# Attention steps of a fused diffusion block: the output products of step k-1 ahead of both transpose rounds of step k

## The chip, the cores and the metric

The kernel runs on one core of a Trainium2 chip, which is one core of eight. The metric is the device time of the whole kernel in microseconds, the median of repeated runs; lower is better. Engines are named as the profile has them: PE is TensorE (PEld its weight loads), DVE is VectorE, ACT is ScalarE, POOL is GpSimd, SP is SyncE, which here only issues DMAs.

## The reference

Two layers over 512 latent tokens with a context of 256 tokens ahead of them, model width 1024, everything in fp32. Each layer projects its normed input, runs two kinds of attention beside each other, joins their outputs in one projection, and then runs a gated feed-forward part with a short convolution. Four kinds of attention occur: in layer 0 MLA (8 heads, latent keys with a rotary part, 768 rows of queries, context included) and SWA (8 heads, window of 128 keys, a sink logit); in layer 1 NA (8 heads, neighbourhood attention on a grid with a relative bias) and GQA (4 heads of 128), both with 512 rows of queries. Cut to what all four share:

```python
s = jnp.einsum('bgrqd,bgkd->bgrqk', q, k_all).astype(jnp.float32) * scale
p = jax.nn.softmax(s, axis=-1)          # SWA: a sink logit more; NA: bias and mask
o = jnp.einsum('bgrqk,bgkd->bgrqd', p, v_all)
```

## The kernel before

The whole program is one launch with an instruction list per engine, written out by hand; semaphores with counted values tie the lists together. Each engine runs its list in order. The change lies in the attention phases, which all come out of the same function, `attention(name, a)`, once on each engine.

**Steps.** A phase works on pairs of heads, and for each pair on units of 128 query rows. A step k is one unit of one pair: MLA and SWA have 4 pairs with 6 units (24 steps), NA 4 pairs with 4 units (16), GQA 2 pairs with 4 units (8). In MLA's units 0, 2, 4 and 5 of a pair all 768 keys are seen (six tiles of 128), in units 1 and 3, which are context rows, only 256 keys. SWA's units see 512, 256, 640, 256, 640 and 512 keys. NA's and GQA's all see 768. The index x is the head within the pair.

**What a step takes, and who does it.**

- Scores, TensorE (`scores`, L1030 in GQA, L1038 elsewhere, L1045 for MLA's rotary part), into PSUM banks 0 to 3, two banks for each head. These banks exist once, so the scores of step k+2 overwrite those of k+1.
- Row minima of the negated scores, VectorE (`minima`, L1866, in NA two passes, L1855 and L1866). They write a copy of the scores to SBUF as well; `mx_done` counts them, and the scores of the next step wait for both of them.
- Exponent with row sum, ScalarE (`exp`, L1442), the reciprocal of the sum, VectorE (L1871), and the scaling of the row, GpSimd (L2180, `p_scaled`).
- Transposes of the scaled probabilities, TensorE (`probs_t`, through `turns`, L993). A round handles one head: its left half of key tiles goes to bank 6, its right half to bank 7. Bank 6 is copied to SBUF by ScalarE (L1425), bank 7 by VectorE (L1830), and the next round's halves wait for `left_free` and `right_free`, each for the copy of its own bank.
- The output product, TensorE (`pv`, L1075), from the transposed probabilities and the values. It waits for both copies of the second round of its step.
- Preparation of the next pair (`prep`): rounds of transposes of q, k and, in MLA and GQA, a third operand, through the same two banks. They follow the transposes of units 1, 2, 3 (MLA), 1, 2 (SWA), 0, 1 (NA) and 0, 1, 2 (GQA).

**The order of the work.** TensorE's list has for step k: scores of k+1, first round of k (x = 0), output product of k-1, second round of k (x = 1), then preparation. At k = 0 there is no output product; after the loop the output product of the last step follows. VectorE's list for the same k is: minima of k+1 for head 0, copy of round (k, 0), minima of k+1 for head 1, reciprocal of k+1 for head 0, (at the first unit of a pair the low part of the finished pair's output), copy of round (k, 1), reciprocal for head 1. ScalarE's: copy of round (k, 0), exponent of k+1 for head 0, (at the first unit of a pair the finished pair's output), copy of round (k, 1), exponent for head 1.

Of the kernel before, what the change touches and what calls it, by code (L numbers as in the profile page):

```python
# [118 lines left out]
def keys_of(unit):  # L119
    _, (a, n), (b, m) = unit  # L120
    return [*range(a, a + n), *range(b, b + m)]


def build(nc, I, C, out):
# [16 lines left out]
    with ctx:  # L141
# [284 lines left out]
        def at_least(eng, sem, value):  # L426

            if not (isinstance(value, int) and value <= 0):
                eng.wait_ge(sem, value)
# [371 lines left out]
        def _(pe):  # L801
# [182 lines left out]
            def attention(name, a):  # L984
# [3 lines left out]
                def turns(r, left, right):  # L988

                    for srcs, b, done, free in ((left, 6, left_done, left_free), (right, 7, right_done, right_free)):  # L990
                        at_least(pe, free, R0 + r)
                        for n, src in enumerate(srcs):
                            last = nc.tensor.transpose(bank(b)[:, n * P:(n + 1) * P], src, ident[:, :])  # L993
                        last.then_inc(done, 1)
# [8 lines left out]
                def prep(p, i):  # L1003
                    what, (left, right) = a.preps[i]
                    if a.name == "mla" and what == "x" and p == 0:
                        turns(a.prep_round[p, i], [x_first[:, t, :] for t in left], [x_first[:, t, :] for t in right])
                        return
                    turns(a.prep_round[p, i], [raw_tile(what, p % 2, t) for t in left],
                          [raw_tile(what, p % 2, t) for t in right])

                def prep_in(p):
                    pe.wait_ge(head_in[p % 2], head_fills[name] + (p // 2 + 1) * a.load_inc)
# [35 lines left out]
                def probs_t(k, x):  # L1048
                    p, u = a.steps[k]
                    n = len(keys_of(a.units[u]))  # L1050
                    pe.wait_ge(p_scaled, S0 + 2 * k + x + 1)
                    v = (sunk if a.name == "swa" else biased)[k % 2][x][:, ROWS - n * P:ROWS]
                    srcs = [v[:, c * P:(c + 1) * P] for c in range(n)]
                    turns(a.unit_round[k, x], srcs[:(n + 1) // 2], srcs[(n + 1) // 2:])

                def pv(k):
                    p, u = a.steps[k]
                    s, t = p % 2, a.units[u][0]
                    keys = keys_of(a.units[u])
                    r = R0 + a.unit_round[k, 1] + 1  # L1060
                    pe.wait_ge(left_free, r)
                    pe.wait_ge(right_free, r)
                    if u == 0:
                        pe.wait_ge(v_in[s], v_fills[name] + (p // 2 + 1) * a.v_inc)
                        at_least(pe, o_lo, OL0 + H0 + (p - 1 if a.name == "na" else p))
                    v = v_raw[s].rearrange("p (t c) -> p t c", t=NT)
                    for c, key in enumerate(keys):
                        for x in range(2):
                            if a.name == "gqa":
                                o, w = bank(4 + x), v[:, key, :]  # L1070
                            else:
                                b = 4 + s if a.name == "na" else 4
                                o = ps[64 * x:64 * x + 64, b * 512:b * 512 + a.acols]
                                w = v[:, key, 0:64] if a.name == "swa" else v[:, key, 64 * x:64 * x + 64]
                            last = mm(o[:, t * P:(t + 1) * P], w, pt[k % 2][x][:, c, :],  # L1075
                                      start=c == 0, stop=c == len(keys) - 1)
                    last.then_inc(pv_done, 1)
# [11 lines left out]
                for k in range(-1, last_step + 1):  # L1089
                    if k < last_step:  # L1090
                        p, u = a.steps[k + 1]
                        if u == 0:
                            pe.wait_ge(left_free, R0 + a.prep_end(p))
                            pe.wait_ge(right_free, R0 + a.prep_end(p))
                        at_least(pe, mx_done, S0 + 2 * (k + 1))
                        scores(k + 1)
                    if k < 0:
                        continue
                    probs_t(k, 0)
                    if k:  # L1100
                        pv(k - 1)
                    probs_t(k, 1)
                    p, u = a.steps[k]
                    for i in range(len(a.preps)):
                        if a.prep_at[i] == u and p + 1 < a.pairs:
                            if i == 0:
                                prep_in(p + 1)
                            prep(p + 1, i)
# [174 lines left out]
            first_norm_turns()  # L1283
            in_projection(0)
            attention("mla", MLA)
            attention("swa", SWA)
            out_projection(0)
            feed_up(0)
            feed_down(0)
            into_projection()  # L1290
            in_projection(1)
            attention("na", NA)
            attention("gqa", GQA)
            out_projection(1)
# [973 lines left out]
```

## Time and profile before

| | us |
|---|---|
| median of 3 runs (lowest, highest) | 1861.03 (1859.75, 1861.37) |
| the profiled execution, its span | 1856.1, 1854.4 |
| TensorE busy, share of the span | 1706.3, 92% |
| VectorE, ScalarE, GpSimd busy | 1019.9, 645.6, 267.3 |
| L993, all transposes through `turns` in attention, matmuls | 141.1 |
| L1171, feed-forward products of layer 0 and 1 | 830.0 in three groups |

The span is the time from the first to the last instruction in the profile; the execution's own time lies 1.7 us above it. The time runs from the input projections of layer 0 (until about 188 us) through MLA (to 316) and SWA (to 411), the feed-forward part of layer 0, the projections of layer 1, NA (1264 to 1354), GQA (to 1421) and the feed-forward part of layer 1. A start in a timeline row is when an instruction began to run on its engine, and rows of one kind that follow each other are merged (x6). For a matmul the duration includes filling and draining of the array, so a merged row ends a little after the next may start; from start to start is the better measure.

### The profile page before, as it was taken

What the parts mean: (1) busy time and instruction counts of PE and PEld (TensorE: products, weight loads), DVE (VectorE), ACT (ScalarE), POOL (GpSimd) and SP (SyncE); (2) the same over time, 40 slices, a digit from 0 to 9 for tenths busy, and PEclk for the clock granted to TensorE, in tenths of its full rate; (3) what the DMA queues carried; (4) which work ended last, traced back from release to release, by engine and by line L of the source; (5) the groups of instructions that cost most, each with busy time, mean ns of one, the idle gap of its engine ahead of it and who ended that gap; (6) DMA issues with size and microseconds to landing.
All of it is one profiled execution on the core that took longest, in us unless ns stands there. A gap on an engine that the chain in (4) does not pass through costs nothing.

```text
span 1854.4 us, 27146 instructions
## 1 busy us (share of the span) xinstructions
PE 1706.3 (92%) x10042; PEld 1366.3 (74%) x10042; DVE 1019.9 (55%) x1927; ACT 645.6 (35%) x1089; POOL 267.3 (14%) x396
## 2 busy tenths in 40 slices
PE   5898898989989999999996969998989799999998
PEld 1876565668878888888785857885667598888886
DVE  3656455754657777776653482156743634443445
ACT  2424455653321212212223332235643433233343
POOL 0414222320200000000010030125521200000001
PEclk9999999999989999999998989998999899999999
DMA  8479441114514343344254542354502523332233
GB/s 300 162 256 322 77 106 44 24 38 158 172 46 121 106 136 116 111 136 126 70 126 116 173 153 96 130 154 104 139 10 80 158 70 90 91 109 72 80 125 136
DMA packets 258270, 224.21 MB, mean 121 GB/s; under 512 B 67484, under 2 KB 218411, under 8 KB 258178
## 3 DMA queue, kind: packets, MB, share of 16 engines
q1 hardware_dynamic: 249156, 202.50, 36.3%
q0 software_dynamic: 7008, 18.79, 3.5%
q10 hardware_dynamic: 2016, 1.71, 0.3%
q8 instruction: 58, 0.95, 0.2%
q14 instruction: 32, 0.26, 0.0%
HBM read 193.71 MB, written 29.25 MB: 120 GB/s over the span
## 4 chain that ended last, share of the span: by engine, by line
PE 80%; DVE 6%; DMA 4%; ACT 3%; issue 3%; SPq 2%; POOL 2%; ACTq 0%; DVEq 0%
PE ps L1171 29%; PE ps L806 10%; PE ps L808 10%; PE ps L807 10%; PE ps L993 5%; PE ps L1075 4%; PE ps L1038 4%; PE ps L1181 1%; DMA w_raw<-in_ffn_down 1%; PE ps L1030 1%; PE ps L863 1%; PE ps L1045 1%; ACT arena L1425 1%; PE ps L1155 1%; DMA wide_raw<-in_ada_w 1%
## 5 line engine op out<-in xcount | busy, mean ns | idle before, releaser
L806 PE MATMUL ps<-w_hi,act_hi 128*128 128x512 f32 (+2 forms) x952 | 370.1, 389 | 21.8 <-DVE act_lo L1614 18.6
L1614 DVE TENSOR_TENSOR w_lo<-w_raw,w_hi 128x2048 fp32r<-128x2048 f32 (+3 forms) x114 | 209.5, 1838 | 310.7 <-ACT w_hi L1316 310.7
L808 PE MATMUL ps<-w_hi,act_lo 128*128 128x512 f32 (+2 forms) x952 | 366.2, 385 | 0.0
L807 PE MATMUL ps<-w_lo,act_hi 128*128 128x512 f32 (+2 forms) x952 | 366.2, 385 | 0.0
L1316 ACT ACTIVATE w_hi<-w_raw 128x2048 fp32r<-128x2048 f32 (+3 forms) x110 | 172.4, 1568 | 308.3 <-PE ps L808 249.2
L1171 PE MATMUL ps<-act_lo,w_hi 128*128 128x512 f32 (+1 forms) x912 | 278.3, 359 | 0.0
L1171 PE MATMUL ps<-act_hi,w_hi 128*128 128x512 f32 (+1 forms) x912 | 277.1, 358 | 0.0
L1171 PE MATMUL ps<-act_hi,w_lo 128*128 128x512 f32 (+1 forms) x912 | 274.6, 355 | 0.0
L806 PEld LDWEIGHTS ps<-w_hi,act_hi 128*128 128x128 f32 x952 | 180.9, 190 | 62.1 <-issue 23.3
L808 PEld LDWEIGHTS ps<-w_hi,act_lo 128*128 128x128 f32 x952 | 180.3, 189 | 34.4
L807 PEld LDWEIGHTS ps<-w_lo,act_hi 128*128 128x128 f32 x952 | 180.6, 190 | 33.5
L1171 PEld LDWEIGHTS ps<-act_hi,w_lo 128*128 128x128 f32 x912 | 151.5, 189 | 27.8
L1171 PEld LDWEIGHTS ps<-act_hi,w_hi 128*128 128x128 f32 x912 | 149.4, 188 | 29.7 <-issue 4.5
L1171 PEld LDWEIGHTS ps<-act_lo,w_hi 128*128 128x128 f32 x912 | 150.7, 189 | 24.6
L993 PE MATMUL ps<-ident,arena 128*128 128x128 f32 x882 | 141.1, 290 | 27.4 <-ACT arena L1425 14.3
L993 PEld LDWEIGHTS ps<-ident,arena 128*128 128x128 f32 x882 | 96.8, 144 | 76.1 <-issue 30.2
L1515 ACT ACTIVATE arena<-ps,conv 128x768 f32<-128x768 f32 (+1 forms) x44 | 39.0, 886 | 313.5 <-PE ps L1171 290.0
L2180 POOL TENSOR_SCALAR arena<-arena,rinv 128x768 f32<-128x768 f32 (+3 forms) x144 | 111.6, 776 | 241.0 <-DVE rinv L1871 241.0
L1669 DVE SCALAR_TENSOR_TENSOR arena<-arena,silu 128x256 f32<-128x256 f32 x336 | 137.1, 478 | 0.9
L1425 ACT ACTIVATE arena<-ps 128x384 f32<-128x384 f32 (+2 forms) x179 | 78.2, 437 | 138.4 <-PE ps L993 135.6
L1442 ACT ACTIVATE arena<-arena,nb 128x768 f32<-128x768 f32 (+4 forms) x144 | 115.4, 801 | 23.8 <-DVE nb L1866 23.3
L1932 DVE SCALAR_TENSOR_TENSOR arena<-ps,conv,arena 128x511 f32<-128x511 f32 x66 | 41.6, 658 | 121.9 <-ACT arena L1515 121.9
(129 smaller groups left out, 2008.2 us busy)
## 6 DMA issues: line engine op xcount, KB each, us to landing
arena<-in_ada_w SPq DMA_DIRECT2D x44, 1024.0 KB, 9.3
w_raw<-in_ffn_up SPq DMA_DIRECT2D x88, 512.0 KB, 5.1
w_raw<-in_ffn_down SPq DMA_DIRECT2D x88, 256.0 KB, 3.0
w_raw<-in_odd_w_in SPq DMA_DIRECT2D x20, 512.0 KB, 4.9
arena<-mods SPq DMA_DIRECT2D x16, 512.0 KB, 7.3
proj_odd<-arena POOLq DMA_DIRECT2D x26, 256.0 KB, 2.7
x_after_mix<-arena SPq DMA_DIRECT2D x10, 512.0 KB, 2.9
arena<-x_after_mix SPq DMA_DIRECT2D x10, 512.0 KB, 5.0
```

The costliest lines, as they stand in the source:

```text
L806: mm(out_, s_hi, m_hi, start=start, stop=False)
L807: mm(out_, s_hi, m_lo, start=False, stop=False)
L808: return mm(out_, s_lo, m_hi, start=False, stop=stop)
L993: last = nc.tensor.transpose(bank(b)[:, n * P:(n + 1) * P], src, ident[:, :])
L1038: last = mm(out_of(x, off, n), qt[s][h, rows], kt[s][h, keys], start=True, stop=not rope)
L1171: last = mm(o, wt[:, k, :], m[:, k, rows], start=st, stop=sp_)
L1316: A(w_hi[:, s, 0:n], w_raw[:, s, 0:n], ACT.Copy).then_inc(w_hi_done, 1)
L1425: A(dst, bank(6, n * P), ACT.Copy).then_inc(left_free, 1)
L1442: A(dst, src, ACT.Exp, bias=nb[:, s, x:x + 1], scale=-1.0, accum_out=rsum[:, s, x:x + 1])\
L1614: V.tensor_sub(out_, full, hi.bitcast(fp32)).then_inc(sem_, 1)
L1669: ins = V.scalar_tensor_tensor(out=ada_sum[:, v, :], in0=w, scalar=x, in1=ada_sum[:, v, :], op0=ALU.mult, op1=ALU.add)
L2180: Q.tensor_scalar(v, v, rinv[:, k % 2, x:x + 1], 1.0, ALU.mult, ALU.mult).then_inc(p_scaled, 1)
```

## The change

In TensorE's list of each attention step the output product of step k-1 moves ahead of the first round of transposes of step k, so that both rounds of step k follow each other. All waits move with the instructions they belong to. The lists of the other four engines are the same, instruction by instruction.

```diff
                         scores(k + 1)
                     if k < 0:
                         continue
-                    probs_t(k, 0)
                     if k:
                         pv(k - 1)
-                    probs_t(k, 1)
+                    for x in range(2):
+                        probs_t(k, x)
                     p, u = a.steps[k]
```

TensorE's list in MLA, the stretch from the short scores of unit 1 to the short scores of unit 3, before. L1038 and L1045 are scores, L993 transposes, L1075 output products (two heads for each key tile).

```order
L1038 MATMUL ps<-arena 128x128 x4
L1045 MATMUL ps<-arena 128x128 x4
L993 MATMUL ps<-ident,arena 128x128 x6
L1075 MATMUL ps<-arena 64x128 x12
L993 MATMUL ps<-ident,arena 128x128 x6
L1038 MATMUL ps<-arena 128x384 x4
L1045 MATMUL ps<-arena 128x384 x4
L993 MATMUL ps<-ident,arena 128x128 x2
L1075 MATMUL ps<-arena 64x128 x12
L993 MATMUL ps<-ident,arena 128x128 x8
L1038 MATMUL ps<-arena 128x128 x4
L1045 MATMUL ps<-arena 128x128 x4
```

The same stretch now:

```order
L1038 MATMUL ps<-arena 128x128 x4
L1045 MATMUL ps<-arena 128x128 x4
L1075 MATMUL ps<-arena 64x128 x12
L993 MATMUL ps<-ident,arena 128x128 x12
L1038 MATMUL ps<-arena 128x384 x4
L1045 MATMUL ps<-arena 128x384 x4
L1075 MATMUL ps<-arena 64x128 x12
L993 MATMUL ps<-ident,arena 128x128 x10
L1038 MATMUL ps<-arena 128x128 x4
L1045 MATMUL ps<-arena 128x128 x4
```

Before, the twelve products stood between two rounds of six transposes; now the two rounds are one run of twelve. In the second step the two short rounds (2 and 2) and a preparation round (6) join to a run of ten.

The end of NA, where the last step has no next scores, before:

```order
L1038 MATMUL ps<-arena 128x512 x2
L1038 MATMUL ps<-arena 128x256 x2
L993 MATMUL ps<-ident,arena 128x128 x6
L1075 MATMUL ps<-arena 64x128 x12
L993 MATMUL ps<-ident,arena 128x128 x12
L1075 MATMUL ps<-arena 64x128 x12
L993 MATMUL ps<-ident,arena 128x128 x6
L1075 MATMUL ps<-arena 64x128 x12
```

The end of NA now:

```order
L1038 MATMUL ps<-arena 128x512 x2
L1038 MATMUL ps<-arena 128x256 x2
L1075 MATMUL ps<-arena 64x128 x12
L993 MATMUL ps<-ident,arena 128x128 x12
L1075 MATMUL ps<-arena 64x128 x12
L993 MATMUL ps<-ident,arena 128x128 x12
L1075 MATMUL ps<-arena 64x128 x12
```

The run of twelve before was the second round of step 14 and the first of step 15. Now the product of step 14 stands between them, and the two rounds of step 15 stand together.

## Rows read from the trace of the kernel before

**Rows 1.** The page's chain that ended last, shares of the span by engine.

```profile
PE 80%; DVE 6%; DMA 4%; ACT 3%; issue 3%; SPq 2%; POOL 2%; ACTq 0%; DVEq 0%
```

**Rows 2.** Busy us (instructions) per engine, the four attention stretches together.

```profile
sum 380.90, PE 344.21 PEld 240.25 DVE 224.22 ACT 207.81 POOL 128.65; mean PE 86.05 PEld 60.06 DVE 56.05 ACT 51.95 POOL 32.16
```

**Rows 3.** Timeline of an MLA step: start us, us, engine, line, operation [idle before].

```profile
225.04 0.88 PE L993 MATMUL ps<-ident,arena 128*128 128x128 f32 x6
...
225.84 1.53 PE L1075 MATMUL ps<-arena 128*64 128x128 f32 x24
...
226.03 0.55 DVE L1830 COPY arena<-ps 128x384 f32<-128x384 f32 x1
226.14 0.94 ACT L1442 ACTIVATE arena<-arena,nb 128x768 f32<-128x768 f32 x1
226.50 0.95 DVE L1866 CUSTOM_DVE_ANT_0 arena<-ps,band 128x768 f32<-128x768 f32 x1
...
227.31 0.88 PE L993 MATMUL ps<-ident,arena 128*128 128x128 f32 x6
...
228.11 0.72 PE L1038 MATMUL ps<-arena 64*128 64x128 f32 x8
228.29 0.56 DVE L1830 COPY arena<-ps 128x384 f32<-128x384 f32 x1 [0.77 <-PE ps L993]
```

**Rows 4.** Timeline, MLA: a preparation round of transposes directly behind T1.

```profile
240.54 0.88 PE L993 MATMUL ps<-ident,arena 128*128 128x128 f32 x6
...
241.73 0.95 PE L993 MATMUL ps<-ident,arena 128*128 128x128 f32 x6 [0.31 <-ACT arena L1425]
```

**Rows 5.** Timeline, start of GQA: the second scores wait for the minima.

```profile
1360.94 0.96 DVE L1866 CUSTOM_DVE_ANT_0 arena<-ps,band 128x768 f32<-128x768 f32 x1 [0.32 <-PE ps L1030]
...
1361.96 2.85 PE L1030 MATMUL ps<-arena 128*128 128x384 f32 x8 [1.06 <-DVE nb L1866]
```

**Rows 6.** Timeline, end of an MLA pair, where the output product is short.

```profile
250.70 0.88 PE L993 MATMUL ps<-ident,arena 128*128 128x128 f32 x6
...
252.09 0.87 PE L993 MATMUL ps<-ident,arena 128*128 128x128 f32 x6
252.16 0.95 DVE L1866 CUSTOM_DVE_ANT_0 arena<-ps,band 128x768 f32<-128x768 f32 x1
...
253.26 1.20 PE L1038 MATMUL ps<-arena 64*128 64x384 f32 x5 [0.29 <-ACT arena L1425]
```

**Rows 7.** Timeline, an SWA step with 512 keys.

```profile
344.17 0.42 DVE L1830 COPY arena<-ps 128x256 f32<-128x256 f32 x1
...
344.68 0.75 DVE L1866 CUSTOM_DVE_ANT_0 arena<-ps,band,arena 128x512 f32<-128x512 f32 x1
...
345.14 0.66 PE L993 MATMUL ps<-ident,arena 128*128 128x128 f32 x4
...
345.72 0.70 PE L1038 MATMUL ps<-arena 64*128 64x256 f32 x4
345.90 0.42 DVE L1830 COPY arena<-ps 128x256 f32<-128x256 f32 x1 [0.39 <-PE ps L993]
```

**Rows 8.** Timeline, an NA step.

```profile
1288.96 0.87 PE L993 MATMUL ps<-ident,arena 128*128 128x128 f32 x6
...
1290.20 0.55 DVE L1830 COPY arena<-ps 128x384 f32<-128x384 f32 x1
...
1290.67 0.68 DVE L1855 CUSTOM_DVE_ANT_0 arena<-ps,arena 128x512 f32<-128x512 f32 x1
...
1292.03 1.56 PE L1038 MATMUL ps<-arena 64*128 64x512 f32 x8
```

**Rows 9.** Transposes (L993): TensorE idle before them until this releaser: us, times.

```profile
  POOL arena L2180: 20.4, 42
```

**Rows 10.** Stretches of 4 us, with granted clock (PEclk) behind the engines.

```profile
1264.00:1268.00 4.00, 2.93 (x8) 1.28 (x8) 0.80 (x2) 1.76 (x2) 4.00 (x2) 0.50 0.02 8
...
1352.00:1356.00 4.00, 2.81 (x34) 2.14 (x32) 1.25 (x2) 1.63 (x5) 0.00 (x0) 1.00 0.04 8
```

## The prediction, as it was put on record

> **What bounds the kernel now.** I read the page's chain by engine first [rows 1]: TensorE carries 80% of the chain that ended last, and the other engines appear in it in small pieces. The change touches one Python loop that four attention phases run, so the second view is the busy table of these four stretches [rows 2]: together 380.9 us, of which TensorE is busy 344.2, or 90%. Attention is TensorE's own time with small gaps; VectorE is busy 224.2 us there (59%), ScalarE 207.8, GpSimd 128.7. No engine beside TensorE is near its limit, so whatever else decides is latency: how long the chain from one TensorE instruction through VectorE or ScalarE back to TensorE takes, and whether TensorE has other work meanwhile.
>
> The third view is the timeline of one step [rows 3]. Name the parts of a step k: S is the scores of step k+1, T0 and T1 the two rounds of transposes of step k, O the output product of step k-1. Before, TensorE runs T0 at 225.04, O at 225.84, T1 at 227.31 and the next S at 228.11. T0 to S is 3.07 us: 0.80 + 1.47 + 0.80, with no gap. What lies beside it: T0's right half is copied by VectorE at 226.03, and behind that copy, in VectorE's program order, stand the row minima of the second head of step k+1, at 226.50. The next S overwrites the banks that these minima read, so it must wait for them. Behind O (1.47 us) both copies and minima are hidden.
>
> **What the change does to a step.** TensorE's instruction count and kinds stay the same; the orders of the other four engines and of all DMAs are unchanged. No wait is added in the code, but two are met in another situation.
>
> First, T1 writes the banks that T0 just filled, so it must wait for ScalarE's copy of T0's left half. Before, O stood between them. How long two rounds need back to back is shown where a preparation round follows T1 [rows 4]: start to start 1.19 us (240.54 to 241.73), against 0.80 for a round without the wait. That is +0.39 per step, the lower price.
>
> Second, and dearer: T0 now starts 1.47 us later, and VectorE, which runs in order, holds the minima of the second head behind T0's copy. From T0 to the next S the chain is: T0's start to VectorE's copy 0.98 us (227.31 to 228.29, where VectorE was free [rows 3]); copy to minima 0.47 us (226.03 to 226.50 [rows 3]); minima to the scores that waited for them 1.02 us (1360.94 to 1361.96 [rows 5]). Sum 2.47 us. Two rounds and their gap need only 1.19 + 0.80 = 1.99 us, so the minima end last and S starts 2.47 us after T0. The step is O 1.47 + 2.47 = 3.94 against 3.07: **+0.87 us**. ScalarE's part of it fits inside: its exponent starts 1.10 after T0 (226.14 less 225.04 [rows 3]) and is 0.94 long, so its second copy starts near 2.1 and nothing on TensorE waits for it unless a preparation round follows.
>
> MLA has 24 steps, 23 of them with an O in the loop (k = 1 to 23). By what step k and step k+1 are (long: 768 keys; short: 256):
> - Long to long with a long O: 3 steps, 3 x 0.87 = 2.6.
> - Long to long with a short O (0.59 us): 4 steps. Here the kernel before already waits: T0 at 250.70, T1 at 252.09 (so O is 1.39 - 0.80 = 0.59), minima at 252.16, S at 253.26, 0.37 after TensorE came free [rows 6]. The row's label names ScalarE's copy, but the code lets this S wait for no such copy, only for the minima, whose end fits too. T0 to S is 2.56; after, 0.59 + 2.47 = 3.06, so +0.50; 4 x 0.5 = 2.0 (the last includes the drain: there the product of the step before now fills the wait for the last scaled probabilities, and two copies become exposed behind it; I count these as equal).
> - Long to short: minima of 256 columns are short, so the lower price rules: 7 x 0.39 = 2.7.
> - Short to long, mostly followed by a preparation round: the preparation needs both ScalarE copies, and between them stands an exponent of 0.94 us [rows 3]. Between 0.39 and 0.87 by the rows above plus this; I take 0.75, nearer the upper end, since minima and exponent are both long ones: 8 x 0.75 = 6.0.
> Sum for MLA 13.3.
>
> SWA: 23 steps. A step with 512 keys on both sides [rows 7]: a round takes 0.58 (345.14 to 345.72), so T0 to S was 1.16 beside O. After: a round's start to its copy is 0.76 (345.14 to 345.90), copy to minima 0.51 (344.17 to 344.68, a sink copy lies between), the minima 0.75 and 0.06 from their end to S as in rows 5: 2.08. Hence +0.92 for the 3 such steps, 2.8. For the rest I carry MLA's prices: 4 steps with a short O at 0.5, halved since these minima are shorter, 1.0; 7 long to short at 0.5 (0.39 and a little for the sink copies), 3.5; 8 short to long at 0.75, 6.0. At the start of each later pair the finished pair's output is evicted by ScalarE and then by VectorE in front of T1's copies. The scores are short here, so O, now first, meets that eviction where T0 took up part of it; 3 x 0.5 = 1.5, an estimate between nothing and 1 us. The drain 0.5. Sum 15.3.
>
> NA: 16 steps, all long, and the minima are two passes [rows 8]: before, T0 at 1288.96, S at 1292.03, 3.07 again. The second head's first pass starts 0.47 after the copy (1290.20 to 1290.67) and S follows 1.36 later (1292.03). After: 0.98 + 0.47 + 1.36 = 2.81, and with O 4.28: +1.21. Of the 15 steps with an O, 9 have no preparation behind them and a next step: 10.9; the last one is the drain, counted as nothing by the same exchange as in MLA. 5 have one: there the kernel before already pays 0.39, and the preparation's right half waits for a copy queued behind the same minima; between 0.82 (1.21 - 0.39) and 1.21 I take 0.95: 4.8. Sum 15.7; 1292.03 is also when TensorE came free, so 1.36 may be a little too long.
>
> GQA: 7 steps with O, one-pass minima like MLA, all long; O is longer but hides more than was needed. At 0.87 to 1.21 I take 1.0: 7.0.
>
> **The sum.** 13.3 + 15.3 + 15.7 + 7.0 = 51.3, with the rows' rounding 52 us. Saved against it: TensorE's waits for GpSimd's scaled probabilities, at most 20.4 us over the whole kernel [rows 9]; most of that is at starts and drains, which the terms above hold. In a step's middle T0 follows S with no gap before ([rows 3]: 225.04), so putting O ahead frees nothing there. Everything behind attention waits for its last output and moves by the same amount. The profiled execution took 1856.1 us (span 1854.4 and 1.7 around it); with 52 it is 1908. The median of the three timed runs is 1861.0, 4.9 above the profiled one, so the forecast is **1913 us**, +2.8%.
>
> **The clock.** A weight on the other side of the sum is TensorE's clock. Rows of this case show it at half its level (0.50, that is 1.2 of 2.4 GHz) at 1264 to 1268, after TensorE was mostly idle, while 1352 to 1356, busy 2.81 of 4 us, ran at full clock [rows 10]. After the change a long step is busy about 5.4 of 6.3 us, 86%, above what kept full clock. The Trainium skill ("TensorE: Matmul & The Clock Gate", A second HAM failure mode: psum-queue depth-cycling) says that short idle spells between groups of matmuls that cycle through PSUM banks can make the clock swing between its two levels. This case's trace does not show it at such gaps.
>
> **The rivals.**
> - The lower price only: VectorE's minima stay hidden and T0 to T1 costs 0.39 in all 68 steps (23 + 23 + 15 + 7): 26.5 us, 1888. For it: the rounds' wait is the only bank conflict that the code shows at first sight. Against it: VectorE's order is fixed and rows 6 show TensorE already waiting for the minima when O is short. Chance 0.10.
> - Faster: the output product fills TensorE's waits for scaled probabilities, and the copies keep pace since VectorE and ScalarE are under 60% busy. Place: S to T0 in every step, and the drains. Price: the 20.4 us of [rows 9] go, and it decides if T1 finds its bank free within the 0.80 us of T0. 1861 - 20 = 1841. Against it: rows 4 show 1.19. Chance 0.02; for it to cancel exactly (no change) 0.02.
> - The clock swings: TensorE's work in attention, 344 us, runs at half clock for a fifth of the time. At half clock a round of fixed length doubles, so 69 us are added to the 52: 1982. Against it the row of 1352. Chance 0.06, and dearer or cheaper in proportion.
> - My forecast, the minima behind the later copy: 0.80. Its own range is 1901 to 1924, from the bounds of the estimated terms: at 0.39 for all 8 short-to-long steps of MLA or of SWA and nothing for SWA's evictions the sum is 47; at 1.0 for the steps of one of the two, 1.21 for all of NA's steps and for GQA's it is 56; and some 7 us more at each end for rows carried from one phase to another and for the median of the runs.
>
> **How the numbers follow.** The range reaches a little towards the first and the third rival: 1895 to 1928. A measurement of this kernel tells about 0.2% (4 us) from no change. Slower: 0.80 + 0.10 + 0.06 = 0.96; within 0.2%: 0.02; faster: 0.02.
>
> **What would show it.** In the changed profile a long MLA step should read O, T0, a gap of 0.4, T1, a gap of about 0.5 ended by the minima (L1866), then S, with S 2.47 us after T0 and a period of 6.3 instead of 5.4 us. VectorE's busy time stays while TensorE's idle time in attention doubles or more, and the four stretches grow by about 13, 15, 16 and 7 us. The first step of each phase keeps its length. Wrong would be: S within 2.1 us of T0 (then VectorE took its copy earlier than I think, and the first rival holds), or a granted clock below 1 in the middle of a phase (the third), or T0 to T1 of 0.80 (the second).

## The result, and the profile after

The changed kernel takes 1917.35 us (median of 4 runs, 1909.91 to 1922.99), the kernel before, on the same chip, 1860.39 (4 runs, 1858.86 to 1861.37). The ratio is 1.030, with a 95% interval of 1.0278 to 1.0321: 57 us slower. The forecast was 1913 us in a range of 1895 to 1928. The profiled execution took 1915.25 us, 59.2 more than that of before. All ratios in this document leave out one run of the kernel before, on the chip of e1, e2, e3 and e5, which took 3389.49 us.

The chain of the changed kernel that ended last, by engine, answers to [rows 1]:

```profile
PE 78%; DVE 7%; DMA 4%; ACT 4%; issue 3%; POOL 2%; SPq 1%; DVEq 0%; ACTq 0%
```

TensorE gives two points to VectorE and ScalarE. How much that is shows in the four attention stretches (MLA, SWA, NA, GQA), with busy us (instructions) of each engine, then the granted clock, the DMA share and GB/s. The last row answers to [rows 2], whose stretches were cut 5.6 us wider than the phases:

```profile
195.06:339.15 144.09, 121.53 (x1123) 79.21 (x1123) 70.25 (x206) 65.00 (x161) 36.77 (x48) 0.97 0.24 56
339.15:447.04 107.89, 83.86 (x724) 56.50 (x724) 62.77 (x217) 56.06 (x154) 31.67 (x48) 0.97 0.09 20
1298.00:1408.46 110.46, 87.53 (x749) 58.92 (x749) 62.22 (x203) 52.15 (x113) 45.69 (x40) 0.94 0.31 80
1408.46:1478.77 70.31, 59.03 (x366) 45.34 (x367) 28.29 (x69) 25.47 (x53) 14.54 (x16) 1.00 0.00 1
sum 432.75, PE 351.94 PEld 239.97 DVE 223.53 ACT 198.68 POOL 128.67; mean PE 87.99 PEld 59.99 DVE 55.88 ACT 49.67 POOL 32.17
```

Cut in the same way, at the first scores of each phase, the kernel before reads 127.50, 91.01, 93.35 and 63.44 us, 375.3 together, with TensorE busy for 340.1 and VectorE for 223.5. The phases grow by 16.6, 16.9, 17.1 and 6.9 us, 57.5 together; all the rest of the span by 1.7. VectorE does the same work. TensorE's idle time in attention goes from 35.2 us (375.3 less 340.1) to 80.8 (432.8 less 351.9), so 45.6 of the 57.5 us are waits. The other 11.9 us are busy time of the same instructions: in part the stretches at half clock that are told below, where scores that take 1.56 us at full clock took 2.93, and the rest is not traced further.

A long MLA step of the changed kernel, from its timeline, answers to [rows 3]: O, T0, T1, S, with the copies and the minima of the second head.

```profile
232.05 1.53 PE L1075 MATMUL ps<-arena 128*64 128x128 f32 x24
...
233.51 0.88 PE L993 MATMUL ps<-ident,arena 128*128 128x128 f32 x6
234.16 0.49 ACT L1425 ACTIVATE arena<-ps 128x384 f32<-128x384 f32 x1 [3.54 <-PE ps L993]
234.49 0.56 DVE L1830 COPY arena<-ps 128x384 f32<-128x384 f32 x1 [1.37 <-PE ps L993]
...
234.79 0.86 PE L993 MATMUL ps<-ident,arena 128*128 128x128 f32 x6 [0.40 <-ACT arena L1425]
234.97 0.95 DVE L1866 CUSTOM_DVE_ANT_0 arena<-ps,band 128x768 f32<-128x768 f32 x1
...
235.98 0.49 PE L1038 MATMUL ps<-arena 64*128 64x128 f32 x4 [0.32 <-DVE nb L1866]
```

The three links of the forecast chain stand there: 0.98 us from T0 to VectorE's copy, 0.48 to the minima, 1.01 to S; together 2.47. T0 to T1 is 1.28 us. VectorE sat idle for 1.37 us before its copy: it waited for T0, which stood behind the whole of O, and had nothing else to do in its order.

An NA step of the changed kernel, from its timeline, answers to [rows 8]:

```profile
1326.25 0.88 PE L993 MATMUL ps<-ident,arena 128*128 128x128 f32 x6
...
1327.23 0.56 DVE L1830 COPY arena<-ps 128x384 f32<-128x384 f32 x1 [1.14 <-PE ps L993]
...
1327.70 0.68 DVE L1855 CUSTOM_DVE_ANT_0 arena<-ps,arena 128x512 f32<-128x512 f32 x1
...
1328.98 1.56 PE L1038 MATMUL ps<-arena 64*128 64x512 f32 x8 [0.58 <-DVE nb L1866]
```

S starts 2.73 us after T0 here, and 2.83 in the step before it (1320.47 to 1323.30). The idle time before the transposes by releaser, over the whole changed kernel, answers to [rows 9]:

```profile
  ACT arena L1425: 59.3, 118
...
  POOL arena L2180: 4.1, 10
```

This view counts TensorE's weight loads together with its matmuls, and a weight load may wait while a matmul still runs; so it is no measure of TensorE's lost time. The matmuls alone stand on the pages, the kernel before first:

```profile
L993 PE MATMUL ps<-ident,arena 128*128 128x128 f32 x882 | 141.1, 290 | 27.4 <-ACT arena L1425 14.3
L993 PE MATMUL ps<-ident,arena 128*128 128x128 f32 x882 | 141.1, 290 | 55.7 <-ACT arena L1425 44.9
```

The transposes themselves waited for ScalarE's copy 32 times before (14.3 us) and 98 times after (44.9 us): T1 met the bank wait 66 times more, for 30.6 us. For GpSimd they waited 5 times before, 3.7 us in all, and 2 times after, 0.5 us; the 20.4 us of [rows 9] are for the greater part weight loads (16.8 in 37 waits). The scores waited for the minima (L1866) 4 times before, 7.6 us, and 28 times after, 19.6 us, and the products for VectorE's copies 3.1 and 7.9 us. So of the new waits the bank is the larger part (30.6 us), the minima behind the late copy the smaller (12.0): where both stand in one step, the minima add only what the bank wait has not already covered.

Last, the clock. Windows of 4 us of the changed kernel at the first step of MLA, in NA's second pair, and at the start of SWA, with columns as in [rows 10]:

```profile
192.00:196.00 4.00, 3.33 (x15) 2.21 (x15) 0.00 (x0) 1.96 (x4) 0.00 (x0) 0.50 1.05 206
...
332.00:336.00 4.00, 2.79 (x35) 2.25 (x33) 1.11 (x2) 0.98 (x2) 0.00 (x0) 1.00 0.01 4
336.00:340.00 4.00, 2.74 (x24) 2.02 (x20) 1.02 (x2) 2.45 (x5) 0.00 (x0) 1.00 0.24 50
340.00:344.00 4.00, 1.94 (x12) 1.02 (x8) 2.45 (x10) 1.80 (x5) 1.39 (x2) 0.87 0.88 196
344.00:348.00 4.00, 3.80 (x15) 1.97 (x16) 1.73 (x8) 1.58 (x6) 0.96 (x2) 0.50 0.00 0
...
1332.00:1336.00 4.00, 2.29 (x16) 1.58 (x16) 2.95 (x9) 3.43 (x8) 3.00 (x2) 1.00 0.33 99
1336.00:1340.00 4.00, 4.00 (x24) 2.19 (x24) 1.33 (x4) 0.04 (x1) 2.94 (x2) 0.57 0.00 0
```

At the start of SWA the granted clock is 0.87 in the stretch from 340 to 344, in which TensorE was busy 1.94 us, and 0.50 (1.2 of 2.4 GHz) in the next. In NA it is 0.57 from 1336 to 1340, behind a stretch with 2.29 us busy. The stretches from 332 to 340, the drain of MLA, busy 2.7 to 2.8 us, ran at full clock.

**Step by step.** From the start of one step's scores to the start of the next one's, in us, read from the timelines. The interval holds these scores and all that follows them to the next; "long O" and "short O" say how long the output product in it is, and the forecast's growth stands beside it. The columns e1 to e7 belong to the experiments below.

| interval | forecast | before | after | e1 | e2 | e4 | e7 |
|---|---|---|---|---|---|---|---|
| MLA, long to long, long O | +0.87 | 5.42 | 6.28 | 5.89 | 5.89 | 5.42 | 5.62 |
| MLA, long to long, short O | +0.50 | 4.91 | 5.49 | 5.30 | 5.01 | 5.30 | 5.28 |
| MLA, long to short | +0.39 | 4.15 | 4.61 | 4.61 | 4.61 | 4.15 | 4.31 |
| MLA, short to long, preparation | +0.75 | 5.81 | 6.51 | 6.52 | 6.20 | 5.82 | 5.95 |
| SWA, 512 keys on both sides | +0.92 | 3.48 | 4.40 | 3.93 | 4.04 | 3.65 | 3.75 |
| NA, no preparation | +1.21 | 4.57 | 5.68 | 5.03 | 5.28 | 4.96 | 5.03 |
| NA, preparation of unit 0 | +0.95 | 6.09 | 7.17 | 7.10 | 7.61 | 6.12 | 6.52 |
| GQA, no preparation | +1.0 | 6.57 | 7.77 | 7.18 | 7.19 | 6.58 | 6.57 |

### The profile page after: what moved, and what is told of

It is laid out like the page before. It is cut to its first block, busy times and chain, and to the rows that moved or that the text cites. A ratio compares the mean times of both kernels' runs of the same rounds, so it can differ in the third digit from the quotient of the medians.

```text
span 1913.6 us, 27146 instructions
## 1 busy us (share of the span) xinstructions
PE 1717.3 (90%) x10042; PEld 1368.8 (72%) x10042; DVE 1019.6 (53%) x1927; ACT 640.2 (33%) x1089; POOL 267.5 (14%) x396
## 4 chain that ended last, share of the span: by engine, by line
PE 78%; DVE 7%; DMA 4%; ACT 4%; issue 3%; POOL 2%; SPq 1%; DVEq 0%; ACTq 0%
PE ps L1171 28%; PE ps L806 10%; PE ps L807 10%; PE ps L808 10%; PE ps L1075 5%; PE ps L993 4%; PE ps L1038 4%; PE ps L1181 1%; DMA w_raw<-in_ffn_down 1%; ACT arena L1425 1%; DVE arena L1830 1%; PE ps L1030 1%; DVE arena L1866 1%; PE ps L1045 1%; PE ps L863 1%
## 5 line engine op out<-in xcount | busy, mean ns | idle before, releaser
L993 PE MATMUL ps<-ident,arena 128*128 128x128 f32 x882 | 141.1, 290 | 55.7 <-ACT arena L1425 44.9
L993 PEld LDWEIGHTS ps<-ident,arena 128*128 128x128 f32 x882 | 96.4, 145 | 95.9 <-issue 62.4
L1830 DVE COPY arena<-ps 128x384 f32<-128x384 f32 (+2 forms) x168 | 79.3, 472 | 100.3 <-PE ps L993 100.0
```

The source lines that it names most:

```text
L1830: V.tensor_copy(dst, bank(7, n * P)).then_inc(right_free, 1)
```

## The experiments

Eight runs on three chips; each ratio is against runs of the kernel before on the same chip (medians there 1863.28 for e1, e2, e3 and e5, 1865.53 for e4, e7 and e8, 1859.61 for e9).

### e1: the changed kernel, VectorE's second minima ahead of its copy of T0

```diff
                     if k < last_step:
                         minima(k + 1, 0)
+                        minima(k + 1, 1)
                     for x in range(2):
                         if k >= 0:
                             probs(k, x)
-                        if x == 0 and k < last_step:
-                            minima(k + 1, 1)
```

> The changed kernel, with one edit on VectorE: the row minima of the second head of step k+1 stand ahead of the copy of the first transpose round of step k, instead of behind it. My theory is that the 57 us lost have two parts: the second round waits for its bank (T0 to T1 1.28 us instead of 0.80), and the next scores wait for minima queued behind a copy that now comes late (T0 to S 2.47 us in MLA, 2.8 in NA). This edit takes away the second part where no preparation round follows: T0 to S should fall to 1.28 + 0.80 = 2.08 us, worth 0.39 in 7 MLA steps, about 0.3 in 12 SWA steps, 0.7 in 9 NA steps and 0.4 in 5 GQA steps, together some 15 us: 1902 (1895 to 1908). Rival 1, only the bank wait counts and the minima are hidden: 1917, no change. Rival 2, the loss is TensorE's clock: the time follows the granted clock and not this edit, 1917 as well. Rival 3, the minima are the whole loss: near 1865.

Measured: 1898.14 us (1896.32 to 1900.57), ratio 1.0187 (1.0170 to 1.0204), inside the 1895 to 1908 expected. By the ratios 22 of the 57 us came back by VectorE's order alone; by the traces the phases shrank by 18.0 us, of which 1.4 are one NA step that ran at half clock in the changed kernel. Its timeline of the long MLA step:

```profile
267.18 0.95 DVE L1866 CUSTOM_DVE_ANT_0 arena<-ps,band 128x768 f32<-128x768 f32 x1
267.65 0.87 PE L993 MATMUL ps<-ident,arena 128*128 128x128 f32 x6
...
268.93 0.86 PE L993 MATMUL ps<-ident,arena 128*128 128x128 f32 x6 [0.40 <-ACT arena L1425]
...
269.72 0.72 PE L1038 MATMUL ps<-arena 64*128 64x128 f32 x8
```

The minima now run beside O, where VectorE was idle, and S follows T1 with no wait: T0 to S is 2.07 us, 1.28 + 0.79. The bank wait of 0.40 is what remains. The table's first row splits so: 6.28 - 5.89 = 0.39 for the minima, 5.89 - 5.42 = 0.47 for the bank. In NA it is 0.65 and 0.46. The short-to-long steps did not move (6.51, 6.52): there the preparation waits for copies, not for the minima. The page of this run has 44.3 us of bank waits before the transposes, where the changed kernel's has 44.9: e1 removes one part and leaves the other.

### e2: the kernel before, the product behind both rounds

```diff
-                    probs_t(k, 0)
+                    for x in range(2):
+                        probs_t(k, x)
                     if k:
                         pv(k - 1)
-                    probs_t(k, 1)
```

> The kernel before, with the output product of step k-1 behind both transpose rounds of step k instead of between them. Both rounds follow each other as in the changed kernel, but T0 starts right after the scores, so VectorE's copy and minima come as early as in the kernel before and lie beside the product. It prices the bank wait alone. My theory: 0.48 us for each step without a preparation round (14 in MLA, of which 4 with a short product at 0.1; 17 in SWA; 10 in NA; 5 in GQA), next to nothing in the 23 with one, since the product then stands where that round waited: 1860 + 20 = 1880 (1874 to 1886). Rival 1, the bank wait is the whole loss: 1917. Rival 3, it costs nothing and the minima are everything: 1861.

Measured: 1891.40 us (1889.71 to 1893.36), ratio 1.0147 (1.0130 to 1.0164). The long MLA step:

```profile
232.47 0.87 PE L993 MATMUL ps<-ident,arena 128*128 128x128 f32 x6
...
233.75 0.86 PE L993 MATMUL ps<-ident,arena 128*128 128x128 f32 x6 [0.41 <-ACT arena L1425]
...
234.55 1.53 PE L1075 MATMUL ps<-arena 128*64 128x128 f32 x24
...
236.01 0.72 PE L1038 MATMUL ps<-arena 64*128 64x128 f32 x8
```

T0 again comes straight behind the scores and the minima are hidden beside O, so this is the bank wait alone: T0 to S is 3.54 us against 3.07, +0.47, as expected. The growth was expected at 20 us and came out at 28 (1891.40 against 1863.28). I had taken the steps with a preparation as free of it, and some are not: MLA's short-to-long ones went from 5.81 to 6.20, while its long-to-short ones with a preparation stayed at 4.55, and GQA's two read 7.62 for 7.73 and 8.70 for 8.70. In NA the steps without a preparation grew by 0.71 and not by 0.47. There the minima are two passes, so VectorE's copy of T0 comes later, and the right half of T1 waits for it too; T1's row is 1.12 us long for 0.86:

```profile
1320.23 0.88 PE L993 MATMUL ps<-ident,arena 128*128 128x128 f32 x6
...
1321.51 1.12 PE L993 MATMUL ps<-ident,arena 128*128 128x128 f32 x6 [0.40 <-ACT arena L1425]
...
1325.26 0.41 PE L993 MATMUL ps<-ident,arena 128*128 128x128 f32 x2 [1.17 <-ACT arena L1425]
```

The last row, the preparation of unit 0 of a pair in NA (6.09 to 7.61), waits for something else again, the order of ScalarE's list, which e8 below shows. So 27 us, by the ratio, is the price of this order in this kernel: the bank wait for the greater part, with these two beside it. It is no price that holds wherever the product stands; e1, with the product ahead and the minima hidden, lies 35 us above the kernel before.

### e3: the change in layer 0 only

```diff
+                    first = a.full
+                    if k and first:
+                        pv(k - 1)
                     probs_t(k, 0)
-                    if k:
+                    if k and not first:
                         pv(k - 1)
                     probs_t(k, 1)
```

> The change in the two attention phases of layer 0 alone (MLA and SWA); NA and GQA keep the order of the kernel before. From the two traces MLA grew by 16.6 us and SWA by 16.9. If the loss is local to each step, as my theory has it, this kernel shows just these: 1860.4 + 33.5 = 1894 (1889 to 1899). A rival in which the slower attention of one layer delays something that the other layer waits for (a transfer, the clock) would leave the sum short or long of that by more than 5 us.

Measured: 1892.94 us (1890.16 to 1895.10), ratio 1.0153 (1.0137 to 1.0170). MLA and SWA took 143.45 and 107.78 us, as in the changed kernel, NA and GQA 93.59 and 63.43, as before. The four phases together are 33.0 us longer than before, and 33.5 were expected. The medians say 29.7 us (1892.94 less 1863.28), some 4 less, just inside the 5 us that the expectation allowed. The loss is local to each phase; nothing in NA, GQA or behind them is seen to give it back or to add to it.

### e4: the kernel before, with e1's order on VectorE

The edit on VectorE is that of e1; TensorE's order is that of the kernel before.

> The kernel before, with VectorE's second minima put ahead of its first copy out of PSUM: the same edit that gave e1 back 19 us, in a kernel whose TensorE order is not changed. Theory (the order of VectorE suits the order of TensorE; with the old TensorE order the minima have 3.07 us of cover and the copy of T0's round is what the next round of the bank waits for): T1's right half waits for a copy that now stands behind both minima, and so does the product; MLA long steps +0.1, MLA short ones +0.6, NA steps +0.6, so 10 to 20 us slower than before, 1871 to 1883. Rival (the minima-first order is better in itself, and e1 tells nothing of the change): 1863 or less, down to about 1845.

Measured: 1875.47 us (1872.64 to 1877.31), ratio 1.0049 (1.0031 to 1.0067), 9 us slower. The rival falls: the minima-first order is no better in itself, it costs 9 us with one order of TensorE and saves 22 with the other. The size lay at the lower edge of the 10 to 20 us that I had expected, since the MLA steps with a long O lost nothing (5.42), and those with a short O and NA's lost 0.39 and not 0.6. Where it bites, an MLA step with a short O:

```profile
227.93 0.55 PE L993 MATMUL ps<-ident,arena 128*128 128x128 f32 x3
...
228.40 0.55 DVE L1830 COPY arena<-ps 128x384 f32<-128x384 f32 x1
...
229.01 0.55 PE L993 MATMUL ps<-ident,arena 128*128 128x128 f32 x3 [0.53 <-DVE arena L1830]
```

The left half of T1 goes, and the right half waits 0.53 us for the copy that now stands behind the minima.

### e5: the kernel before, the product in two halves around T1

If two rounds with nothing between cost 0.4 us, the round of a preparation that follows T1 costs that in the kernel before too [rows 4]. Here half of the product stands between them. Only steps with a preparation are cut, and not the first of a pair; `pv` takes the first or the second half of the key tiles.

```diff
+                    p, u = a.steps[k]
+                    parted = p + 1 < a.pairs and u in a.prep_at[:len(a.preps)] and u > 0
                     probs_t(k, 0)
                     if k:
-                        pv(k - 1)
+                        pv(k - 1, 0 if parted else None)
                     probs_t(k, 1)
+                    if k and parted:
+                        pv(k - 1, 1)
```

> The kernel before, with one edit: in the steps that a preparation round follows (20 with an output product and not the first of a pair) the product of step k-1 is cut in two halves by key tiles, one between T0 and T1, one between T1 and the preparation. By the theory, what stands between two rounds hides the 0.39 us wait for the copy; the kernel before leaves that wait open in front of each preparation. Half a long product is 0.73 us, more than 0.39, half a short one 0.3. Expected gain 0.2 to 0.39 us for each of the 20, less where ScalarE's exponent holds up its second copy: 3 to 8 us, 1855 (1852 to 1858). Rival (the wait in front of a preparation is hidden by something else, or VectorE's queue sets it): 1860, no change.

Measured: 1856.41 us (10 runs, 1852.75 to 1860.93), ratio 0.9972 (0.9962 to 0.9982). A parted MLA step (L1078 is the product's line in this kernel):

```profile
235.63 0.44 PE L993 MATMUL ps<-ident,arena 128*128 128x128 f32 x2
236.00 0.88 PE L1078 MATMUL ps<-arena 128*64 128x128 f32 x12
236.80 0.48 PE L993 MATMUL ps<-ident,arena 128*128 128x128 f32 x2
237.22 0.88 PE L1078 MATMUL ps<-arena 128*64 128x128 f32 x12
238.07 0.85 PE L993 MATMUL ps<-ident,arena 128*128 128x128 f32 x6
238.84 0.71 PE L1038 MATMUL ps<-arena 64*128 64x128 f32 x8
```

No wait is left, and T0 to S is 3.21 us against 3.46. The same in the table's terms: short to long with a preparation 5.81 to 5.55, and long to short with a preparation 4.54 to 4.42.

### e7: half of the product ahead of T0, half between T0 and T1

```diff
+                    if k:
+                        pv(k - 1, 0)
                     probs_t(k, 0)
                     if k:
-                        pv(k - 1)
+                        pv(k - 1, 1)
                     probs_t(k, 1)
```

> After, but every output product is cut in two by keys: half of it is issued ahead of T0 and half between T0 and T1, and nothing between T1 and the scores. Theory (the loss has two parts: nothing between the two rounds, so T1 waits 0.39 us and more for the copies of T0's banks, and nothing between T1 and S, so S waits for T0 to minima, 2.47 us in MLA and 2.83 in NA): half a product of 0.74 us covers the bank wait whole, and T0 to S of 2.34 us of TensorE's own work nearly meets the 2.47 us chain; MLA about +4, SWA +5, NA +6, GQA +2 against before, total about 1880 (1872 to 1890). Rival A (what counts is that T0, and with it the copies and minima, starts late behind any part of a product): about half of the whole loss stays, 1889 or more. Rival B (only the bank wait matters): 1866 or less.

Measured: 1884.37 us (1882.41 to 1886.33), ratio 1.0103 (1.0085 to 1.0120). The phases grew by 4.8, 6.9, 5.9 and 0.4 us. Both rivals fall. With half a product between them T0 and T1 start 1.61 us apart with no bank wait. In the step of the table's first row T0 starts at 229.39 and S at 231.85, 2.46 us, near the forecast's 2.47. TensorE's own work between them is 2.41 us, so only 0.05 of this is the chain through the minima. The +0.20 of the interval is half a product (0.81) ahead of T0, and 2.46, against 3.07 before; 0.15 of it is the cut itself, since two halves of 0.81 us stand where a whole product took 1.47. In MLA this run therefore says little about the chain. In NA it says more:

```profile
1331.70 0.87 PE L993 MATMUL ps<-ident,arena 128*128 128x128 f32 x6
...
1334.43 1.56 PE L1038 MATMUL ps<-arena 64*128 64x512 f32 x8 [0.24 <-DVE nb L1872]
```

T0 to S is 2.73 us, the same as in the changed kernel, with no bank wait and with 2.41 us of TensorE's own work; the scores wait for the minima (L1872 in this kernel).

### e8: e5 also at the first step of a pair

The condition `u > 0` of e5 is dropped.

> e5 (before, with the product cut in two around T1 where a preparation follows) extended to the first step of a pair, which e5 left whole; only NA and GQA prepare there, 7 and 3 times. Theory (T1 to the preparation is 1.28 us there and would be 0.80 if half a product stood between): 0.4 us a time, 4 us less than e5, so about 0.9955 of before (1853 where before is 1861). Rival (the preparation's own copies on ScalarE set the length of these steps): the same as e5, 0.997 of before.

Measured: 1865.08 us (12 runs, 1861.20 to 1870.66), ratio 1.0000 (0.9989 to 1.0011). Neither the theory's 0.9955 nor the rival's 0.997: these steps became longer, 7.04 us against 6.09 in NA. There are two of them with a product, where I had written seven: NA has four pairs, so three preparations, and the first falls into a step with no product. What the changed wait hangs on shows in ScalarE's rows of such a step, of e5 first:

```profile
1294.25 0.60 ACT L1466 ACTIVATE act_hi<-ps 128x512 fp32r<-128x512 f32 x1
1294.78 0.49 ACT L1433 ACTIVATE arena<-ps 128x384 f32<-128x384 f32 x1
```

and of e8, with the second half of the product and the preparation on TensorE:

```profile
1303.10 0.88 PE L1078 MATMUL ps<-arena 128*64 128x128 f32 x12
...
1305.14 0.41 PE L993 MATMUL ps<-ident,arena 128*128 128x128 f32 x2 [1.17 <-ACT arena L1433]
```

```profile
1304.02 0.60 ACT L1466 ACTIVATE act_hi<-ps 128x512 fp32r<-128x512 f32 x1 [0.95 <-PE ps L1078]
1304.51 0.48 ACT L1433 ACTIVATE arena<-ps 128x384 f32<-128x384 f32 x1
```

At the first step of a pair ScalarE's list has the output of the finished pair (L1466) ahead of the copy of T1 (L1433). The output needs the product's last half, which now comes behind T1, so ScalarE waits 0.95 us for it and T1's copy waits with it; then the preparation waits 1.17 us for that copy. This is the same fault as in the change: an instruction put behind another on TensorE delays, through the order of a second engine, something that did not depend on it. The 2.9 us that e8's trace has more than e5's in MLA do not come from the edit: there both run the same instructions, and e8's first long step ran at half clock (the scores at 205.66 took 2.93 us instead of 1.56). The two longer steps explain 1.9 us, 0.1%; the ratio lies 0.28% above that of e5, and what makes up the rest is not shown.

### e9: e5 once more

> The kernel of e5 once more, with runs of the kernel before on the same chip, since e8, which runs the same instructions in MLA and SWA, took 2.9 us more in MLA (its first step ran at half clock) and its ratio was 1.000. Theory (the parted product saves 0.4 us a pair in MLA and about as much in NA and GQA, some 3 us in all, and e8 lost it in NA, where ScalarE's copy of T1 came 1.2 us late behind the output of the pair): 0.9985 of before (0.997 to 0.9995). Rival A (0.9972 of e5 was the edit's own doing): 0.9972 again. Rival B (e5's gain was the clock's luck): 1.000.

Measured: 1857.44 us (12 runs, 1850.23 to 1860.51), ratio 0.9984 (0.9972 to 0.9996). The theory's value, but its working was too low: step by step e5 and e9 agree within 0.02 us behind the first steps of the phases, and against before they save 0.56 us in each of three MLA pairs (0.25 + 0.12 + 0.19, and not 0.4), 0.3 in SWA, 1.0 in NA (three parted steps) and 1.3 in GQA (7.73 to 7.01 and 8.71 to 8.09). That is 4.3 us, or 0.9977, which lies in the intervals of both e5 and e9. Rival B falls; rival A is not excluded, since 0.9972 is the edge of this run's interval. The parted product is the one version here that beats both kernels, by some 0.2%, at the edge of what can be told.

## Why the prediction was right

**The chain through the minima held, link by link.** The first rows of the table are the forecast's terms: +0.86 for +0.87, +0.58 for +0.50, +0.46 for +0.39, +0.70 for +0.75, SWA's +0.92 exactly. NA came out at +1.11 to +1.20 for +1.21 (from the first pass of the minima to S it took 1.28 us in the step shown, for 1.36), and its steps with a preparation at +0.86 and +1.08 for +0.95. GQA was +1.10 to +1.20 in the steps without a preparation and +0.74 in those with one, for +1.0 throughout. e1 and e7 show the cause and not only the size: take the minima from behind the copy and MLA's 0.39 goes; take the bank wait away and NA's 2.73 stays.

**Bank wait.** It was carried at 1.19 us from start to start and is 1.28 in every long step, so 0.47 where 0.39 stood. [Rows 4] measured a preparation behind T1; why that is 0.09 shorter was not tried. In the long-to-long steps this did not matter, since the minima end later; in the seven long-to-short steps of MLA it is the term that was too small, by 0.07 each. The two short-to-long steps of MLA's last pair, which no preparation follows, were carried at 0.75 with the others and grew by 1.02.

**The sum.** Forecast 51.3 us, measured 57.5. Of this, 5.6 us are set apart, taken from intervals where the order of the work is the same in both kernels, or where one step stands out from its fellows; all of them overlap a stretch at half clock: MLA's first two intervals +2.24, SWA's first +0.06, SWA's next +1.35 (6.95 us, against 5.32 in the later pairs, less the 0.28 by which it stood out before), NA's first +0.49, one NA step +1.43 (8.32 against 6.69, less 0.20). The rest is 51.9: MLA 14.4 for 13.3, SWA 15.5 for 15.3, NA 15.2 for 15.7, GQA 6.9 for 7.0. That SWA and GQA come so near is in part luck. In SWA the evictions at the start of a pair, carried at 3 x 0.5 us on top of 7 long-to-short steps at 0.5, did not show: these seven grew by 3.7 us in all, for 5.0. Against that the three steps with a short product and a next step grew by 0.59 each for 0.25, and the eight short-to-long ones by some 6.4 us for 6.0. In GQA the steps with a preparation were too dear and the others too cheap. The profiled execution lay 7 us above the 1908 of the forecast, and the median 4 above 1913.

**What was said and did not hold.** "The first step of each phase keeps its length": MLA's first interval took 6.60 us for 4.50, at half clock in the windows above. e4, with TensorE's old order, shows 6.25 there and e7, with a new one, 4.50, so this is not the change's doing. The SWA start is less clear. Its second interval took 4.90 us before, 5.4 to 5.5 in e5, e8 and e9, 5.75 in e4, 6.14 in e7, and 6.4 to 7.5 in e1, e2, e3 and after. It is longer the more of it falls at half clock: 1.2 us of it before (until 327.8), 4.4 in the changed kernel (343.0 to 349.8 is at 0.50). Whether the change's idler drain of MLA brings that on is not shown: e4 and e9, which keep TensorE's old order in the drain, were at 0.50 for as long as the changed kernel (330.9 to 337.5 and 326.0 to 332.5). And one of the prediction's own signs of being wrong, a granted clock below 1 in the middle of a phase, did appear, in one NA step (0.57 from 1336 to 1340, +1.43 us).

The drains fit the sum, but not by the links that it names. From the last scores of NA to the first of GQA the time went from 14.61 to 15.86 us. This stretch holds steps 14 and 15, which the forecast carried at 1.21 and 0; in MLA the same stretch grew by 0.43, for 0.50 and 0. In step 14 no further scores follow, so the minima cannot hold them up. NA's last two steps on TensorE, in the changed kernel:

```profile
1396.83 0.86 PE L993 MATMUL ps<-ident,arena 128*128 128x128 f32 x6 [0.40 <-ACT arena L1425]
1398.90 1.53 PE L1075 MATMUL ps<-arena 128*64 128x128 f32 x24 [1.21 <-DVE arena L1830]
...
1401.64 0.86 PE L993 MATMUL ps<-ident,arena 128*128 128x128 f32 x6 [0.40 <-ACT arena L1425]
1403.32 0.95 PE L1075 MATMUL ps<-arena 128*64 128x128 f32 x13 [0.81 <-DVE arena L1830]
```

The products wait 1.21 and 0.81 us for the copy of T1, since no scores come between them. The 0.81 stands in the kernel before too (at 1352.97), and there the first round of the last step waits 0.92 us for GpSimd's scaled probabilities (at 1349.02), which the earlier product now fills, as the prediction said. The first wait has another cause than the minima, so that its 1.21 us equal their term is luck.

**The rivals.** The lower price only (1888) describes what e1 and e2 left over: 1898 and 1891, so even its world was priced too low, for the 0.47 and the steps with a preparation. The faster one was priced from [rows 9] at 20.4 us, most of which are weight loads; the transposes' own waits for GpSimd were 3.7 us, so this was the most that it could bring, and T1 did not find its bank free. Of the clock that swings, the trace shows, besides the starts of MLA and NA, which are at half clock in the kernel before too, a longer stretch of it at the start of SWA and one NA step: some 3 us in 433, and not 69. MLA's 86% busy steps kept full clock. The Trainium skill ("TensorE: Matmul & The Clock Gate", A second HAM failure mode: psum-queue depth-cycling) says of another kernel, whose matmul groups cycle through PSUM banks, that its short idle spells were frequent enough for the clock to swing. Here the transposes waited for their bank 98 times, 44.9 us in all, and this trace agrees at most for the NA step behind the stretch with 2.29 of 4 us busy, which holds three such waits (0.41, 0.92 and 0.38 us). In e2 the same step holds waits of 1.17 and 0.31 us, and the clock stayed at 1.00.

## What to carry to other kernels

In this kernel two rounds through the same PSUM banks needed other work of TensorE between them, at least as long as the copy's return (0.47 us more than the round's own 0.8), and that work should stand between them rather than ahead of both. When an instruction is moved on one engine, read the in-order lists of the others for what is queued behind its consumer: a copy 1.5 us later held back minima that did not need it, and a product 0.8 us later held back a copy. The best order on one engine depends on that of the next, so an edit that costs 9 us alone may save 22 beside another.

## What the runs showed of the hardware that was not expected

The time of one and the same program goes in most sets with the mean granted clock of the run: the changed kernel's four runs were 1909.91 us at 0.970, 1915.25 at 0.967, 1919.44 and 1922.99 at 0.963, and e9's reached from 1850.23 at 0.971 to 1860.51 at 0.966. e7's four, 1882.41 to 1886.33 us at 0.965 to 0.966, show no such order. A single profile is therefore no measure for a few microseconds, and neither is a phase that begins with a clock fall. The interval of one kind of step in mid-phase is such a measure: NA's without a preparation is 4.56 to 4.58 us in each of the five traces whose NA leaves it as it was (before, e3, e5, e8, e9).
